# Second layer's feed-forward of a two-block model: nine column panels as seven half-size products instead of eight

## What is computed

```python
def swiglu(t, w_in, w_out):
    a, b = jnp.split(t @ w_in, 2, axis=-1)
    return (jax.nn.silu(a) * b) @ w_out

x = x + g2 * swiglu(modulate(rmsnorm_2(x, norm2_g[i]), sh2, sc2), ffn_w_in[i], ffn_w_out[i])
```

## Time and profile before

| what | us |
| --- | --- |
| median of the runs | 2569.47 |
| the runs | 2567.28, 2569.47, 6536.11 |
| the profiled execution, its own time | 2569.75 |
| its span, first to last instruction | 2568.4 |
| PE busy in the span | 2527.7 |
| DVE, ACT, POOL busy | 1456.3, 954.7, 128.7 |
| second feed-forward, PE's first to last matmul | 359.36 |

### The profile page before, as it was taken

How to read it: one execution, slowest core, us unless ns; L and a number is a source line. 1 busy time by engine, 2 the same in 40 slices (tenths; PEclk the granted TensorE clock), 3 DMA queues, 4 the chain that set the end, 5 groups by cost and what they waited for, 6 DMA issues and landing times.

```text
span 2568.4 us, 34037 instructions
## 1 busy us (share of the span) xinstructions
PE 2527.7 (98%) x14253; PEld 2111.1 (82%) x14253; DVE 1456.3 (57%) x2442; ACT 954.7 (37%) x1775; POOL 128.7 (5%) x140
## 2 busy tenths in 40 slices
PE   8999999999999999999999999999999999999998
PEld 6888888888888778888888987888888888888887
DVE  6786644444566347766565188576734644533434
ACT  5442223453445443332532277432323323322222
POOL 0000000000010010000022000100000101000001
PEclk9999999999999999999999999999999999999999
DMA  4220002212234145464222100365522222222221
GB/s 144 82 83 19 24 33 78 99 66 82 101 114 163 66 148 181 171 224 162 99 75 94 55 1 17 107 230 213 213 99 82 99 99 98 87 101 93 98 95 70
DMA packets 39514, 267.29 MB, mean 104 GB/s; under 512 B 4288, under 2 KB 4544, under 8 KB 9024
## 3 DMA queue, kind: packets, MB, share of 16 engines
q1 hardware_dynamic: 30064, 206.71, 22.6%
q0 software_dynamic: 8608, 57.18, 6.2%
q10 hardware_dynamic: 688, 1.22, 0.1%
HBM read 263.00 MB, written 2.10 MB: 103 GB/s over the span
## 4 chain that ended last, share of the span: by engine, by line
PE 92%; DVE 5%; ACT 2%; issue 1%; DMA 0%; DVEq 0%; SPq 0%; ACTq 0%
PE bank L142 90%; PE bank L145 2%; DVE w_lo L151 1%; ACT tmp L148 1%; DVE tmp L159 0%; DVE x_t L159 0%; DVE dd L151 0%; DMA x_t<-in_x_t 0%; ACT L148 0%; DVE heads_t L159 0%; DVE change L159 0%; ACT w_hi L148 0%; DVE tmp L151 0%; DVE change L151 0%; DVE da_stat L168 0%
## 5 line engine op out<-in xcount | busy, mean ns | idle before, releaser
L142 PE MATMUL bank<-h_hi,w_hi 128*128 128x512 f32 (+1 forms) x1992 | 764.3, 396 | 1.4 <-ACT h_hi L148 1.2
L142 PE MATMUL bank<-h_lo,w_hi 128*128 128x512 f32 (+1 forms) x1992 | 742.6, 391 | 1.0 <-DVE h_lo L159 1.0
L142 PE MATMUL bank<-h_hi,w_lo 128*128 128x512 f32 (+1 forms) x1992 | 630.1, 391 | 0.0
L151 DVE TENSOR_TENSOR w_lo<-w_raw,w_hi 128x512 fp32r<-128x512 f32 (+3 forms) x746 | 495.7, 722 | 188.7 <-ACT w_hi L148 188.1
L148 ACT ACTIVATE w_hi<-w_raw 128x512 fp32r<-128x512 f32 (+3 forms) x746 | 424.9, 638 | 309.4 <-PE bank L142 299.8
L142 PEld LDWEIGHTS bank<-h_hi,w_hi 128*128 128x128 f32 (+1 forms) x1992 | 374.0, 188 | 82.1 <-issue 4.8
L142 PEld LDWEIGHTS bank<-h_lo,w_hi 128*128 128x128 f32 (+1 forms) x1992 | 373.8, 188 | 80.5 <-DVE h_lo L159 1.5
L142 PEld LDWEIGHTS bank<-h_hi,w_lo 128*128 128x128 f32 (+1 forms) x1992 | 372.7, 188 | 76.8 <-issue 1.8
L142 PE MATMUL bank<-f_hi,w_hi 128*128 128x512 f32 x672 | 261.6, 389 | 0.2 <-DVE w_lo L151 0.2
L142 PE MATMUL bank<-f_lo,w_hi 128*128 128x512 f32 x672 | 247.8, 389 | 0.0
L142 PE MATMUL bank<-f_hi,w_lo 128*128 128x512 f32 x672 | 225.9, 389 | 0.0
(11 more groups left out here) (337 smaller groups left out, 3004.6 us busy)
## 6 DMA issues: line engine op xcount, KB each, us to landing
w_raw<-in_pack_ffn SPq DMA_DIRECT2D x60, 1024.0 KB, 4.8
ada_w<-in_ada_w POOLq DMA_DIRECT2D x48, 1024.0 KB, 5.2
w_raw<-in_pack_mlp SPq DMA_DIRECT2D x32, 1024.0 KB, 4.9
w_raw<-in_pack_gdn_qkv SPq DMA_DIRECT2D x12, 1024.0 KB, 4.9
w_raw<-in_pack_sc_cu SPq DMA_DIRECT2D x8, 1024.0 KB, 4.8
w_raw<-in_pack_ffn SPq DMA_DIRECT2D x8, 768.0 KB, 4.2
w_raw<-in_pack_gdn_z SPq DMA_DIRECT2D x4, 1024.0 KB, 4.8
w_raw<-in_pack_gate_a SPq DMA_DIRECT2D x4, 1024.0 KB, 4.9
```

Source lines behind the costliest of these rows:

```text
L142: return self.engine.matmul(*a, **k) if self.engine is not None else self
L151: return self.engine.tensor_tensor(*a) if self.engine is not None else self
```

## The change

Panels 5, 7, ..., 21 of `ffn1_1` (`by_seven`) are computed another way. The panel is seen as two column halves by two feature halves (quarters a11, a12, a21, a22 of 128x512), the input as two feature halves by two token halves. Where a plain product of such 2 x 2 blocks takes eight products of blocks, this one takes seven, with sums and differences of weight quarters (s1 to s4) and of input quarters (t1 to t4), and additions of the results. Each product is 4 x 3 matmuls over 256 tokens. In detail:

- Once, when h is ready, POOL adds `h_hi` + `h_lo` to `h_sum` (eight of 128x512); DVE makes t1 to t4 (four of 128x1024), ACT rounds them, DVE makes their rests (`t_pool`, `t_vector`, `t_scalar`).
- Per seven panel DVE makes s1 to s4 in the panel before (`seven_sums_vector`); ACT and DVE split seven pieces in place of four, three of them while the panel runs. The copies of w_hi and w_lo are now a ring of eight slots of 128x512, each free when what was eight before it is used.
- ACT copies each of the first four products out of PSUM after it ends, with a split piece or two between (`seven_scalar`); POOL adds up three times 128x256 (`seven_pool`); DVE adds the rest from PSUM to "lower" (b's columns) and "upper" (a's), then tanh, product and rounding as before.
- Even panels, and those behind a block's first, take their two groups one after the other.

All panels of the first feed-forward and all else stay.

```diff
+    SEVEN_KEYS, SEVEN_FIRST = ("ffn1_1",), 5
+    SLOTS = 8
+    first_loose = min(number[key, 0, 0] for key in SEVEN_KEYS)
+
+    def by_seven(n):
+        key, _, i = order[n]
+        return key in SEVEN_KEYS and i >= SEVEN_FIRST and i % 2 == 1
+
...
 
+    QUARTERS = {"a11": (0, 0), "a12": (0, 1), "a21": (1, 0), "a22": (1, 1)}
+    SEVEN = ("a11", "s1", "s3", "s2", "s4", "a22", "a12")
...
+    def split_hi_loose(S, n, i):
+
+        S.wait_ge(*loaded(f"raw_loaded{n % 2}", n // 2 + 1))
+        if by_seven(n) and SEVEN[i][0] == "s":
+            S.wait_ge(*at("dve_seven", (n, SEVEN[i])))
+        S.wait_ge(*at(*slot_held[slot_at[n] + i - SLOTS]))
+        S.activation(loose_room(w_hi, n, i), loose_source(n, i), ACT.Copy).then_inc(
+            *up("act_hi", (n, i), *([n] if i == n_pieces(n) - 1 else [])))
+
+    def split_lo_loose(V, n, i):
+        V.wait_ge(*at("act_hi", (n, i)))
+        V.tensor_tensor(loose_room(w_lo, n, i), loose_source(n, i), loose_room(w_hi, n, i).bitcast(F32),
+                        ALU.subtract).then_inc(
+            *up("dve_lo", (n, i), *([n] if i == n_pieces(n) - 1 else [])))
+
...
@@ -502,7 +597,7 @@
             _, nk, width = where[key][block][i]
             if token_tiles:
                 groups = [[m] for m in range(token_tiles)]
-            elif i == first and width == 2 * P and not (key == "gdn_qkv" and i):
+            elif i == first and width == 2 * P and not (key in ("gdn_qkv", *SEVEN_KEYS) and i):
                 groups = [[0, 1]]
             else:
                 groups = [[c] for c in range(width // P)]
...
+    def seven_sums_vector(V, n):
+
+
+        sums = (("s1", "a21", "a22", ALU.add), ("s3", "a11", "a21", ALU.subtract), ("s2", "s1", "a11", ALU.subtract),
+                ("s4", "a12", "s2", ALU.subtract))
+        V.wait_ge(*loaded(f"raw_loaded{n % 2}", n // 2 + 1))
+        for name, first, second, op in sums:
+            for part in (first, second):
+                if part[0] == "s":
+                    V.wait_ge(*at("dve_seven", (n, part)))
+            side = lambda part: s_quarter(part) if part[0] == "s" else raw_quarter(n, part)
+            V.tensor_tensor(s_quarter(name), side(first), side(second), op).then_inc(*up("dve_seven", (n, name)))
+            yield
...
+    TOKEN_SIDE = ("b11", "t1", "t3", "t2", "b22", "t4", "b21")
+    READ_FIRST = {3: 0, 5: 1}
+
...
+    def seven_tensor(T_, rings, key, i):
+
...
+        left, right = TOKEN_HALVES
+        outs = (both[:, left], lower[:, right], third[:, left], both[:, right], upper[:, right], lower[:, left],
+                upper[:, left])
+        emptied = {0: before_both, 1: before_lower, 2: before_third, 4: before_upper}
+        for j, (out, name) in enumerate(zip(outs, TOKEN_SIDE)):
+            if j in emptied:
+                T_.wait_ge(*freed(emptied[j]))
+            if j in READ_FIRST:
+                T_.wait_ge(*at("act_seven", ("open", n, READ_FIRST[j])))
+            T_.wait_ge(*at("act_hi", (n, j)))
+            w_of = lambda tiles_, k: slot(tiles_, n, j)[:, k * P:(k + 1) * P]
...
+                x_hi, x_lo, ready = token_side(name, k)
+                if ready is not None:
+                    T_.wait_ge(*ready[0])
+                    T_.wait_ge(*ready[1])
+                T_.matmul(out, w_of(w_hi, k), x_hi, start=(k == 0), stop=False)
+                T_.matmul(out, w_of(w_hi, k), x_lo, start=False, stop=False)
+            T_.wait_ge(*at("dve_lo", (n, j)))
+            for k in range(4):
+                done = T_.matmul(out, w_of(w_lo, k), token_side(name, k)[0], start=False, stop=(k == 3))
+            if j < 6:
+                done.then_inc(*up("pe_seven", (n, j)))
+            else:
+                done.then_inc(*up("pe_seven", (n, j), ("panel", n)))
+        T_.step()
+
+    def seven_scalar(S, key, i, pair_read):
+
+        n = number[key, 0, i]
+        both, lower, third = (bank_of((key, 0, i, name)) for name in ("both", "lower", "third"))
+        left, right = TOKEN_HALVES
+        copies = ((sums_pair[i // 2 % 2][:, left], both[:, left]), (open_pair[i // 2 % 2][:, left], lower[:, right]),
+                  (open_pair[i // 2 % 2][:, right], third[:, left]), (sums_pair[i // 2 % 2][:, right], both[:, right]))
+        for j in range(7):
+            if 1 <= j <= 4:
+                S.wait_ge(*at("pe_seven", (n, j - 1)))
+                if j == 1 and pair_read is not None:
+                    S.wait_ge(*at(*pair_read))
+                S.activation(*copies[j - 1], ACT.Copy).then_inc(
+                    *up("act_seven", ("open", n, j - 1), frees=(key, 0, i, {3: "third", 4: "both"}[j]) if j > 2 else None))
+            if 1 <= j <= 3:
+                split_hi_loose(S, n, PIECES + j - 1)
+            if 0 <= j - 3 < n_pieces(n + 1):
+                split_hi_loose(S, n + 1, j - 3)
+        S.step()
+
+    def seven_vector(V, key, i):
+
+        n = number[key, 0, i]
+        for j in range(7):
+            if j == 6:
+                tile = (key, 0, i, "lower")
+                V.wait_ge(*at("pe_seven", (n, 5)))
+                V.wait_ge(*at("pool_seven", ("last_two", n)))
+                halves = lambda whole: whole[:, :].rearrange("p (a b) -> p a b", a=2)
+                V.tensor_tensor(halves(open_pair[i // 2 % 2]),
+                                open_pair[i // 2 % 2][:, TOKEN_HALVES[1]][:, None, :].to_broadcast([P, 2, PW]),
+                                halves(bank_of(tile)), ALU.add).then_inc(*up("dve_seven", ("lower", n), frees=tile))
+            if 1 <= j <= 3:
+                split_lo_loose(V, n, PIECES + j - 1)
+            if 0 <= j - 3 < n_pieces(n + 1):
+                split_lo_loose(V, n + 1, j - 3)
+        V.step()
+
+    def seven_upper(V, key, i):
+
+
+        n, tile = number[key, 0, i], (key, 0, i, "upper")
+        V.wait_ge(*at("pe_seven", (n, 6)))
+        V.wait_ge(*at("pool_seven", ("last_two", n)))
+        V.tensor_tensor(sums_pair[i // 2 % 2][:, :], sums_pair[i // 2 % 2][:, :], bank_of(tile)[:, :], ALU.add).then_inc(
+            *up("dve_seven", ("upper", n), frees=tile))
+
+    def seven_pool(G, key, i):
+
+        n = number[key, 0, i]
+        left, right = TOKEN_HALVES
+        sums, pair = sums_pair[i // 2 % 2], open_pair[i // 2 % 2]
+        G.wait_ge(*at("act_seven", ("open", n, 3)))
+        G.tensor_tensor(sums[:, right], sums[:, right], sums[:, left], ALU.add).then_inc(
+            *up("pool_seven", ("two", n)))
+        G.wait_ge(*at("pool_seven", ("two", n)))
+        G.tensor_tensor(pair[:, right], pair[:, right], sums[:, right], ALU.add).then_inc(
+            *up("pool_seven", ("three", n)))
+        G.wait_ge(*at("pool_seven", ("three", n)))
+        G.tensor_tensor(sums[:, right], sums[:, right], pair[:, left], ALU.add).then_inc(
+            *up("pool_seven", ("last_two", n)))
+        G.step()
...
+    T_ORDER = (0, 2, 1, 3)
+
+    def t_pool(G, norm):
+
+        all_of(G, ("act_h_hi", (norm.name, DT - 1)), ("dve_h_lo", (norm.name, DT - 1)))
+        for k in range(DT):
+            G.tensor_tensor(h_sum[:, k, :], h_hi[:, k, :].bitcast(F32), h_lo[:, k, :].bitcast(F32), ALU.add).then_inc(
+                *up("pool_seven", ("h", k)))
+
+    def t_vector(V):
+
+        b11, b12, b21, b22 = h_quarter(0, 0), h_quarter(0, 1), h_quarter(1, 0), h_quarter(1, 1)
+        made = {0: (b12, b11, None, 3), 2: (b22, b12, None, 7), 1: (b22, t_raw(0), 0, 7), 3: (b21, t_raw(1), 1, 7)}
+        for n, i in enumerate(T_ORDER):
+            first, second, after, last = made[i]
+            V.wait_ge(*at("pool_seven", ("h", last)))
+            if after is not None:
+                V.wait_ge(*at("dve_seven", ("t", after)))
+            V.tensor_tensor(t_raw(i), first, second, ALU.subtract).then_inc(
+                *up("dve_seven", ("t", i), *(["raw_done"] if n == 3 else [])))
+            yield
+        for i in T_ORDER:
+            V.wait_ge(*at("act_seven", ("t_hi", i)))
+            all_of(V, ("dve_seven", "raw_done"))
+            V.tensor_tensor(t_lo[:, i, :], t_whole[:, i, :], t_hi[:, i, :].bitcast(F32),
+                            ALU.subtract).then_inc(*up("dve_seven", ("t_lo", i)))
+            yield
+
+    def t_scalar(S):
+        for i in T_ORDER:
+            S.wait_ge(*at("dve_seven", ("t", i)))
+            S.activation(t_hi[:, i, :], t_whole[:, i, :], ACT.Copy).then_inc(*up("act_seven", ("t_hi", i)))
+            yield
 
     WIDE = 2 * PW
 
...
                 else:
                     S.wait_ge(*at("dve_ffn", ("product", layer, blk, f)))
                     S.wait_ge(*at(*hidden_before(layer, blk)))
                     S.activation(f_hi[:, f, :], y[:, :], ACT.Copy).then_inc(*up("act_ffn", ("hi", layer, blk, f)))
-            gemm_scalar(S, f"ffn1_{layer}", take_hidden, panels=(k0, k0 + nk))
+            key = f"ffn1_{layer}"
+            steps = t_scalar(S) if blk == 0 and key in SEVEN_KEYS else iter(())
+            for first, last, seven in ffn_runs(layer, k0, nk):
+                if not seven:
...
```

(34 more changed lines are left out.)

132 lines of the change are left out of this document (120 added, 12 removed).

## The result

The changed kernel takes 2573.9 us (median, 2571.2 to 2575.2) against 2569.4 for the kernel before: ratio 1.002, 95% interval 1.0012 to 1.0027. By 2% that is the same time, but the interval leaves out 1: it is slower by 3 to 7 us. Its profiled execution took 2574.31 us with a span of 2573.0. The forecast was 2573.0. One of the thirteen executions of the kernel before took 6536.11 us, for a reason not known; the median is not moved by it.

The account below looks back on a forecast made before the run. PE, busy 98% of the span, was taken to bound the kernel. The terms -8.0 + 0.8 + 4.0 + 5.1 + 0.5 + 0.7 = +3.1 on 2569.75 gave 2572.9, say 2573 us; range 2562 to 2585.

Parts of the forecast that it names:

- The saving: On PE, nine panels of 84 half-size matmuls at 0.119 us take 10.00 instead of 10.89 each: -8.0 us.
- Exclusion of DVE and POOL: Shared SBUF ports: whichever comes second waits, 1.16 us into a POOL instruction or 0.55 into a DVE one, alternating.
- Stall A: Panel 1: POOL's h_sum additions hold up DVE's w_lo, so PE waits: +0.8 us.
- Stall B: Panel 3: DVE's preparation delays the product of panel 1 and then ACT's w_hi, so PE waits: +4.0 us.
- restart: PE begins 0.14 us after what it waited for; at some seven stalls about +0.7 us is left over.
- Stall C: Block ends, seven panels 7, 15 and 21: PE waits for w_lo or "lower", with a growing lag: +5.1 us.
- The pair's chain: DVE and ACT's chain per pair of panels: 21.5 us where PE needs 20.9, so each pair falls behind by 0.6.
- Inside the blocks: Second block: 0.5 us of the lag over its pairs stalls PE before the block's end: +0.5 us.
- POOL's 128x256 addition: In seven panels, one such addition taken as 0.70 us, between 0.11 and 1.29; about 1.05 with its wait.
- R1: Gain kept, DVE wins its turns and the stalls vanish: 2562 us; 2568 if only block-end waits stay; chance 0.18.
- R2: In seven panels POOL's short additions cost a whole one, 1.29 us, decisive from 0.65 on: 2588 us; chance 0.19.
- R3: In seven panels half-size matmuls run at their load, 0.188 us each, 15.8 a panel: 2620 us; chance 0.03.

Follow-up runs that it names:

- spread run: The changed kernel with DVE's eight 1024-column t instructions and ACT's roundings issued one every six steps instead of in a block: 2568.2 us, ratio 0.9995 to the kernel before.
- one-addition run: The changed kernel with POOL's first two of three additions per seven panel left out, results lacking two terms: 2570.1 us, ratio 1.0001 to the kernel before.

## Why the prediction was right

The changed kernel's profiled execution is 4.6 us above that of before, where the sum was +3.1. All signs held, and all places but two (nothing was lost inside the blocks, and the clock was not foreseen). That the number fits so well is in part luck: in the stage itself 5.5 were lost, not 3.1. The saving came 0.6 short and the clock took 2.85 that no term held, while the stalls were 1.1 cheaper than forecast and this execution reached the stage 1.0 sooner. Step by step:

- **The saving, -8.0: came as -7.4.** A half-size matmul steps at 10.07 / 84 = 0.1199, as forecast 0.119; the difference of 0.0009 times 84 times 9 is 0.7. The 378 of the earlier trace rows counts every matmul that overlaps the window; only 375 start in it, and 45.00 / 375 = 0.120 is the step. The term multiplies the error by 756.
- **Exclusion of DVE and POOL: right, alternation included.** A w_lo that waits for POOL was taken as 0.69 + 1.10 = 1.79. The eight of panels 1 and 2, shortest, median and longest in ns:

```profile
L151 DVE TENSOR_TENSOR w_lo<-w_raw,w_hi x8: 678/1776/1791, 2205.0 to 2218.8; 128x512 fp32r<-128x512 f32 x8
```

In the run with h_sum on DVE the same eight took 684 ns each. That the two tmp reading a bank kept 1.48 beside POOL's additions agrees with what the Trainium skill says ("SBUF — State Buffer", SBUF: two separate sides): against GpSimd the lock is taken by a DVE instruction in a 2-port mode or with two SBUF inputs; each tmp here has one.

- **Stall A, +0.8: a wait of 0.44,** and panel 1 lasts 0.75 longer.
- **Stall B, +4.0: +3.8.** The chain DVE product, ACT f_hi, ACT w_hi held link by link: the product's end was forecast 34.7 us after the stage's start and came 34.4 after it (its start 33.7). Shown by the spread run, which removes it without removing any work.
- **Missing: the clock, +2.85 in panel 3.** I gave the price of a stall as its length and a restart of some 0.1 each. After 3.65 us without a matmul PE ran 13 matmuls at 0.427. This is the step that failed, the price of B, which is 6.6 in all and not 4.0. The sum shows only part of it, since the other stalls were too dear (A, B, C, in-block and restart: 11.1 forecast, 10.0 found), while the saving was 0.6 too high.
- **Stall C, +5.1: +5.0,** at the three places, 1.6, 2.3 and 1.1 against 1.5, 2.2 and 1.5 (5.2 as they stand). The pair's chain was worked out as 21.5; it is 21.33 (POOL's first additions start at 2372.35 and 2393.68), against PE's 10.07 + 10.91 = 20.98. The one-addition run takes C away but for 0.6.
- **Inside the blocks, +0.5: no wait,** only 0.03 in each of six even panels. The lag grew more slowly, by 0.35 per pair and not 0.6.
- **POOL's 128x256 addition:** taken as 0.70, about 1.05 with its wait; recorded 0.93 and 1.07. How long one takes with nothing beside it no run shows. Three of them with their hops take 3.2 to 3.4, as forecast (3.3), but 0.70 itself was a guess halfway between two ends, and that it came out is luck.

Of the rivals, R1 said that if only C stays the time is 2568: the spread run is nearly that kernel, at 2568.2, with A's 0.4 left. R2 was too dear, its additions of 1.29 did not come. Nor does its "from 0.65 on" follow: by the forecast's own chain, 21.5 against PE's 20.9 with three additions in it, the pair falls behind from 0.50 on. R3's step of 0.188 did not come either.
